# The causal mask of the second attention moves from TensorE to VectorE, and the row maxima are kept with their sign turned

## The reference

```
c = jnp.cumsum(log_f, axis=1)                      # one running sum per head
s = einsum('bhqd,bhkd->bhqk', qi, k) * scale       # scale = 1/8
s = s + cqi[..., None] - c[:, :, None, :]
s = jnp.where(kpos[None, :] <= qpos[:, None], s, -jnp.inf)
pr = jax.nn.softmax(s, axis=-1)
o = einsum('bhqk,bhkd->bhqd', pr, v)
```

## Time and profile before

| | |
|---|---|
| median of 3 runs | 2521.71 us (2521.15 to 2522.60) |
| time of the profiled execution | 2520.34 us |
| its span | 2518.6 us |
| PE busy | 2474.5 us, 98% |
| PEld busy | 2018.5 us, 80% |
| DVE busy | 1531.5 us, 61% |
| ACT busy | 1099.5 us, 44% |
| POOL busy | 1327.1 us, 53% |

### The profile page before, as it was taken

One profiled execution on the slowest core, in us unless ns is written; L12 is line 12 of the kernel. 1 busy time (PEld: TensorE's weight loads), 2 busy tenths in 40 slices (PEclk: granted clock), 3 DMA queues, 4 the chain that ended last, 5 costly groups with the idle time before them and its releaser, 6 DMA issues. The chain is left out here.

```text
span 2518.6 us, 36344 instructions
## 1 busy us (share of the span) xinstructions
PE 2474.5 (98%) x11658; PEld 2018.5 (80%) x11658; DVE 1531.5 (61%) x2240; ACT 1099.5 (44%) x2018; POOL 1327.1 (53%) x1092
## 2 busy tenths in 40 slices
PE   8999999999999999999999999999999999999999
PEld 5788888888788878888888888777778888878787
DVE  5455552344777775435656566655668777776785
ACT  4332333301766651126777777732433333344432
POOL 3788887433455554431111111154279888666683
PEclk9999999999999999999999999999999999999999
DMA  3222223579210015321111111331133333486552
GB/s 110 88 71 67 71 67 109 179 259 327 78 34 25 29 37 177 134 93 59 43 42 42 42 42 42 111 133 51 39 116 113 121 117 109 137 275 212 181 184 80
DMA packets 126502, 267.27 MB, mean 106 GB/s; under 512 B 13872, under 2 KB 14000, under 8 KB 126400
## 3 DMA queue, kind: packets, MB, share of 16 engines
q1 hardware_dynamic: 84800, 157.85, 19.5%
q10 hardware_dynamic: 41600, 108.19, 12.0%
HBM read 198.02 MB, written 67.96 MB: 106 GB/s over the span
## 5 line engine op out<-in xcount | busy, mean ns | idle before, releaser
L641 POOL TENSOR_SCALAR whi<-raw 128x512 fp32r<-128x512 f32 x194 | 146.8, 757 | 810.9 <-PE bank L869 402.6
L643 POOL TENSOR_TENSOR wlo<-raw,whi 128x512 fp32r<-128x512 f32 x194 | 273.0, 1407 | 16.2
L806 PE MATMUL bank<-a_hi,whi 128*128 128x512 f32 x464 | 184.8, 398 | 3.7 <-POOL wlo L643 2.0
L806 PE MATMUL bank<-b_lo,whi 128*128 128x512 f32 x464 | 183.3, 395 | 0.0
L656 POOL TENSOR_TENSOR wlo<-a,whi 128x512 fp32r<-128x512 f32 x114 | 166.5, 1460 | 12.9 <-ACT whi L1693 12.2
L869 PE MATMUL bank<-b_hi,whi 128*128 128x512 f32 x384 | 156.9, 409 | 0.0
L869 PE MATMUL bank<-b_hi,wlo 128*128 128x512 f32 x384 | 151.6, 395 | 0.0
L869 PE MATMUL bank<-b_lo,whi 128*128 128x512 f32 x384 | 151.2, 394 | 0.0
L806 PE MATMUL bank<-b_hi,whi 128*128 128x512 f32 x336 | 133.3, 397 | 0.4 <-DVE b_lo L2311 0.4
L806 PE MATMUL bank<-a_hi,wlo 128*128 128x512 f32 x336 | 132.6, 395 | 0.0
L806 PE MATMUL bank<-a_lo,whi 128*128 128x512 f32 x336 | 132.5, 394 | 0.0
(11 more groups left out here) (710 smaller groups left out, 7630.1 us busy)
## 6 DMA issues: line engine op xcount, KB each, us to landing
raw<-in_w SPq DMA_DIRECT2D x206, 256.0 KB, 2.6
a<-in_pairs SPq DMA_DIRECT2D x152, 256.0 KB, 2.6
wd_scr<-wd SPq DMA_DIRECT2D x55, 256.0 KB, 5.1
wd<-in_down SPq DMA_DIRECT2D x44, 256.0 KB, 4.5
xs_scr<-made ACTq DMA_DIRECT2D x40, 256.0 KB, 2.5
fc<-c_scr ACTq DMA_DIRECT2D x16, 512.0 KB, 3.7
h_scr<-up_y ACTq DMA_DIRECT2D x13, 512.0 KB, 2.6
raw<-wd_scr SPq DMA_DIRECT2D x26, 256.0 KB, 2.7
```

What stands on the lines that cost most here:

```text
L641: nc.gpsimd.tensor_scalar(hi, src, 1.0, 1.0, ALU.mult, ALU.mult).then_inc(w_hi, 1)
L643: nc.gpsimd.tensor_tensor(lo, src, hi.bitcast(F32), ALU.subtract).then_inc(w_lo, 1)
L806: last = nc.tensor.matmul(psum_ap, ws[w][:, k, :], a[:, kt, hs(h)], start=(first and i == 0 and j == 0), stop=(final and i == n - 1 and j ...
```

## The change

The mask matmul is left out of `scores`. In `maxima`, DVE first copies a block of large negative numbers (`never`) into the last 128 columns of the scores in PSUM wherever the mask, read as an integer, is not zero (`later_keys`), signals `fx.masked` and waits for it, and then runs the combined operation. That operation now forms minus the score times scale plus `c`, and gathers the minimum, which is the negated maximum. So it writes `neg_max` itself, and the small operation behind it goes. ScalarE's exp gets `scale=-1.0`. The sum `c` is stored with its sign turned once, ahead of the attention, by an operation that was there. The semaphore `fx.max` goes, and its waits on PE and ACT are on `fx.neg_max`. The wait of `maxima` for the transposes of step `s - 3` goes too.

```diff
@@ scores(s) on TensorE
-                    pe.wait_ge(fx.max, st + max(s - 1, 0))
+                    pe.wait_ge(fx.neg_max, st + max(s - 1, 0))
                     for c in range(0, w, HALF):
                         n = min(HALF, w - c)
                         ks = slice(c, c + n)
                         dst = score[s % 2][:, ks]
                         nc.tensor.matmul(dst, f_q[pp][hh][:, q], f_k[pp][hh][:, ks], start=True, stop=False)
-                        if c + n == w:
-                            nc.tensor.matmul(score[s % 2][:, w - P:w], ident_r[:], mask_r[:, P:2 * P], start=False, stop=False)
                         mm = nc.tensor.matmul(dst, f_q[pp][hh][:, q], f_klo[pp][hh][:, ks], start=False, stop=True)
@@ expo(s) on ScalarE
-                    nc.scalar.activation(fp[s % 3][:, 0:w], fp[s % 3][:, 0:w], ACT.Exp, bias=neg_max[:, one],
+                    nc.scalar.activation(fp[s % 3][:, 0:w], fp[s % 3][:, 0:w], ACT.Exp, bias=neg_max[:, one], scale=-1.0,
@@ on ScalarE, ahead of sums_in
-                        act.wait_ge(fx.max, st + (8 if s == 9 else 16))
+                        act.wait_ge(fx.neg_max, st + (8 if s == 9 else 16))
@@ on VectorE
+            later_keys = mask_r[:, P:2 * P].bitcast(mybir.dt.int32)
+            never = mask_r[:, 2 * P:3 * P].bitcast(F32)
@@ maxima(s) on VectorE
-                    dve.wait_ge(fx.flipped, ch + (CHUNKS_OF[s - 3][-1] + 1 if s >= 3 else 0))
                     dve.wait_ge(fx.scored, st + (s + 1))
                     settle()
+                    v.copy_predicated(score[s % 2][:, w - P:w], later_keys, never).then_inc(fx.masked, 1)
+                    dve.wait_ge(fx.masked, st + (s + 1))
+                    settle()
 
                     v.tensor_tensor_reduce(out=fp[s % 3][:, 0:w], in0=score[s % 2][:, 0:w], in1=fc[hh][:, 0:w],
-                                           scale=SCALE, scalar=-3.0e38, op0=ALU.subtract, op1=ALU.max,
-                                           accum_out=mx[:, one]).then_inc(fx.max, 1)
-                    dve.wait_ge(fx.max, st + (s + 1))
-                    v.tensor_scalar(neg_max[:, one], mx[:, one], -1.0, None, ALU.mult).then_inc(fx.neg_max, 1)
+                                           scale=-SCALE, scalar=3.0e38, op0=ALU.add, op1=ALU.min,
+                                           accum_out=neg_max[:, one]).then_inc(fx.neg_max, 1)
@@ the running sums, once
-            v.tensor_scalar(fp1[0:16, :], fp0[0:16, :], 1.0 / SCALE, None, ALU.mult).then_inc(chain_step, 1)
+            v.tensor_scalar(fp1[0:16, :], fp0[0:16, :], -1.0 / SCALE, None, ALU.mult).then_inc(chain_step, 1)
```

More of the change, by code:

```diff
@@ L160, in __init__ @@
         self.scored = sem(n + "_scored")
-        self.max = sem(n + "_max")
         self.neg_max = sem(n + "_neg_max")
@@ L179, in __init__ @@
         super().__init__(sem, n)
+        self.max = sem(n + "_max")
         self.q_sq = sem(n + "_q_sq")
@@ L189, in __init__ @@
         self.g_out = sem(n + "_g_out")
+class ForgetSemaphores(AttentionSemaphores):
+    def __init__(self, sem, n):
+        super().__init__(sem, n)
+        self.masked = sem(n + "_masked")
 STEPS = [(hh, qb) for hh in range(2) for qb in range(NB)]
@@ L408, in build @@
         n0, n1, n2 = NormSemaphores(sem, "n0"), LayerNormSemaphores(sem, "n1"), LayerNormSemaphores(sem, "n2")
-        sw, fx = WindowSemaphores(sem, "sw"), AttentionSemaphores(sem, "fx")
+        sw, fx = WindowSemaphores(sem, "sw"), ForgetSemaphores(sem, "fx")
         chain_step = sem("chain_step")
```

## The result

The changed kernel takes 2533.44 us (median of 5 runs, 2531.59 to 2539.07), the kernel before 2521.71 (2520.86 to 2523.78). The ratio is 1.0043, with a 95% interval of 1.0032 to 1.0054: slower by about 11 us. The forecast was 2519.1 within 2511 to 2527.

What follows compares the result with a forecast made beforehand. TensorE's queue was taken to bound seven of eight pairs, the last partly ScalarE and VectorE. Gains of 4.1 us less 1.0 at turns and 0.5 in the last pair gave 2.6: 2521.71 becomes 2519.1 us, range 2511 to 2527.

Steps and rivals of the forecast that it cites:

- TensorE's part: 128 mask matmuls leave TensorE's queue at 0.11 us each: 14.1 us, or 12.3 for seven pairs, 1.76 to a pair.
- Its give-back: Freed TensorE time lost again to longer waits at `values`; with the longer maxima, 1.17 us of a pair's 1.76.
- the delay of `maxima`: On VectorE, copy 0.28 plus hand-over 0.09 less sign operation 0.19: maxima ends 0.18 us later, bounds 0.06 and 0.30.
- Three `maxima` on the path: In each of seven pairs three delayed maxima lie on TensorE's path; the delay's bounds move the forecast 2.5 us either way.
- the way to `values(5)`: VectorE's chain to this weight load holds two maxima, +0.36 us; TensorE arrives 0.33 earlier, so the wait grows by 0.69.
- The sum for a full pair: Of 1.76 us freed in a pair, 1.17 is lost to waits: net gain 0.6 us, 4.1 for seven pairs.
- The turns and the last pair: Loop turns lose 0.5 us each, -1.0; the last pair about -0.5, between a gain of 1 and a loss of 2.
- The third: Rival: VectorE's copy becomes the path in most steps, 23 us against 14.1 saved, 9 us slower, 2530.7 us; chance 0.15.
- Its point of decision: VectorE-copy rival decides once more than 78 of 128 maxima are on the path, or 47 with a 0.30 us delay.
- The second: Rival: the masks' time comes through in seven pairs, 10 us gained, 2511.7 us (2508 to 2516); chance 0.33.
- the fourth: Rival: mask hidden under weight loads, so removal frees only 0.06 us each; 2 us slower, 2523.7 us; chance 0.08.
- TensorE's clock: Granted in full in the stage but for the last pair, 0.97; any loss from longer waits was left outside the sum.

Runs made afterwards that it cites:

- the kernel with the old maxima: Kernel before with the mask matmul left out, nothing in its place and the maxima step unchanged: 0.9977 of the kernel before.
- the kernels without a mask: Changed kernel without the predicated copy, so no mask on either engine, sign turned: 2516.57 us against 2523.31, 0.9973 of the kernel before.
- the two adds: Changed kernel with an add for the copy, and that add repeated behind a wait: 2564.48 and 2563.93 us, 1.0159 of the kernel before.
- the split with eight steps: Against the kernel before: sign turned, mask an add ahead of the reciprocal in steps 0-3, 11, 13-15, a matmul elsewhere; 0.9980 and 0.9979 of it.
- the split with four steps: Against the eight-step split: add only in steps 11 and 13 to 15, steps 0 to 3 a matmul again; 0.9983 of the kernel before.
- the kernel with the add: Changed kernel with a tensor_tensor add of the mask in place of the predicated copy: 1.0019 of the kernel before.

## Why the prediction was wrong

- **TensorE's part.** The price of a mask was right: 0.11 us by the starts. Its give-back was too small. I counted about 0.6 us of a pair's 1.76 (0.33, 0.11 and most of twice 0.1) as lost to waits by masks alone; it was 0.86 (the kernel with the old maxima).
- **The step that failed: the delay of `maxima`.** I took 0.18 us, from a copy of 0.28 and a hand-over of 0.09. The row that I took the 0.09 from, the combined operation behind the reciprocal, isn't a hand-over: the one doesn't wait for the other's result. The hand-over is 0.19, the copy 0.30, and from copy to combined operation 0.49. Against the 0.19 for the sign operation that is 0.30, the upper bound that I had given, and it holds for the short copies only. In steps 2 and 3 of a pair the copies meet GpSimd and take 0.56 and 0.96 us (in step 10 about 0.35). The sum put this term at nothing, with the words "nothing on GpSimd's queue moves", and no bound of mine held it; it is 0.70 us to a pair.
- **Three `maxima` on the path.** The count was near (2.8, from the kernels without a mask and with one add), but it isn't fixed, as the two adds show, and I multiplied it with too small a delay. It is also not a count of the two `maxima` on the way to `values(5)`, since that wait did not grow: 0.19 us where it had been 0.26 and I had said 0.9 (`values` for `add`, in all: 2.9 us where it was 3.4). I had named this as a sign that the masks' time comes through, and it didn't. The wait that set the time was another, that of the transposes for `low`, 5.4 us before and 17.8 after, and the sum has no term for it.
- **The sum for a full pair.** The kernels in between give it: masks out -0.90, sign operation out -0.19, an add's 0.49 us in +1.35, the copy in the add's place +0.70: 0.96 us slower, where I had 0.6 faster. Seven pairs make 6.7 us. Against my sum the 1.55 us between the two are 0.23 for what the masks give back (0.86 for 0.63), 0.62 for the delay of `maxima` (1.35 less 0.19, for 3 x 0.18) and 0.70 for the copies that meet GpSimd.
- **The turns and the last pair.** At a turn TensorE waits 3.37 us where it waited 2.35; I had said 2.9. The halves with a turn took 42.6 where they took 41.7, 1.8 us together. The second half of the seventh pair, which ends in the last one, took 39.78 us where it took 39.08; this I didn't follow. The last pair took 3.5 us more, where I had 0.5. One copy there, of 1.40 us beside an operation of GpSimd of 2.39 us, is likely the largest part: with adds in place of all the copies the last half takes 28.99 us and not 31.02, and it took 27.97 before.

```profile
1649.77 2.39 POOL L649 TENSOR_TENSOR wlo<-raw,whi 128x512 fp32r<-128x512 f32 x1
...
1650.92 1.40 DVE L2514 COPY_PREDICATED score<-mask_r 128x128 f32<-128x128 int32 x1
...
1653.50 0.94 ACT L1570 ACTIVATE fp<-fp,neg_max 128x768 f32<-128x768 f32 x1 [1.67 <-DVE neg_max L2518]
```

- **The whole.** From the first score to the last transpose the stage takes 13.2 us more: 6.7 for the seven pairs, 1.8 in the halves with a turn, 0.5 more in those behind a turn, 0.7 at the seventh pair's end and 3.5 in the last pair. In the profile the changed kernel came to the stage 1.6 us earlier, and its whole span is 11.2 us longer.
- **The rivals.** The third, VectorE's copy as the path, came nearest and was given 0.15. Its full price was 2530.7 us, and the kernel is slower than that, but not in its way: exp waits in 60 of 128 steps, and the delay counts 2.8 times to a pair and not 16. Its point of decision, 78 `maxima` on the path or 47 at the larger delay, was the wrong measure, since the masks' 14.1 us never came through. The second, that they come through, is excluded by the kernel with old maxima; the fourth by the starts.
- **TensorE's clock.** In the sum it was left open, and it is part of the loss. The stretches behind both turns at half clock:

```profile
1284.63:1288.04 3.41, 3.23 (x10) 2.67 (x11) 1.77 (x5) 1.02 (x3) 0.66 (x1) 0.50 0.44 146
1417.75:1421.16 3.41, 3.41 (x12) 2.72 (x12) 1.86 (x5) 1.57 (x5) 0.25 (x1) 0.50 0.35 120
```

The granted clock is 0.50 there, 1.2 GHz, where the kernel before had 1.00 behind its turns. In the kernel with old maxima and no mask the half behind each turn took 25.2 us where its other first halves took 23.85: 1.3 us for each such stretch. In the changed kernel it is only 0.2 to 0.3 us, likely because VectorE's chain sets that half anyway. The last pair has more of it too, as the lines of the kernel before and of the changed one show:

```profile
1609.83:1613.24 3.41, 3.41 (x13) 2.96 (x14) 2.92 (x7) 3.06 (x7) 0.00 (x0) 0.50 0.02 5
```

```profile
1615.72:1622.54 6.82, 5.06 (x16) 4.25 (x17) 4.00 (x11) 5.79 (x11) 0.00 (x0) 0.50 0.17 51
```

What twice as long at half clock can cost there is seen in the split with eight steps: its last pair's first half took 27.95 us with 3.4 us at half clock in one profile and 29.12 with 6.8 in the other, of the same kernel. How much of the changed kernel's 3.5 us it is stays open.

Open is also why the clock falls behind some turns and not behind others. The waits there were 2.35 and 2.47 us in the kernel before (it didn't fall) and 2.06 and 2.11 in the split with four steps (it fell both times); behind 2.81 us at the second turn of the kernel with the add it didn't. So the length of the wait alone doesn't tell.

## What to carry to other kernels

Before moving work from a full engine to one with idle time, list all waits of the full engine, its weight loads' too, and follow them back through the other. If that engine's operation stands between two others that already just make it, the freed time is given back as longer waits, and the added one is paid on top. A pair of kernels settles it: the work left out of the one engine with nothing in its place, and the work on both. The move may pay in some steps of a loop and not in others: here the splits by step were the only versions with masks on VectorE that gained, and about half of what they gained is the sign operation's.

## What the hardware showed that I had not expected

- A predicated copy of 128 x 128 with both inputs in SBUF takes 0.30 us alone, and 0.35 to 1.40 where it meets an operation of GpSimd; it ends about 0.15 us after that one. With 512 columns and only the mask in SBUF it took at most 0.70 us, beside GpSimd too. An add with the scores from PSUM and only the mask from SBUF takes 0.28 to 0.30 us in every one of 128 cases.
- Behind such a copy or add, the combined operation starts 0.19 us after its end when it waits for it.
- Stretches of 3.41 us at half clock came behind turns of the loop with waits of TensorE of 2.1 to 3.7 us, and not behind others of 2.3 to 2.8.
